# Two units of an input projection moved into the stage that prepares its input

## The reference, cut to what matters

```
u = _rmsnorm(h, w['g_mix'][i])                     # 1536 tokens x 1024
proj = u @ w['w_in'][i]                            # columns: q, k, v, z, xbc, dt
q, k, v, z, xbc, dt = jnp.split(proj, [o1, o2, o3, o4, o5], axis=-1)
...
gates = jax.nn.sigmoid(u @ w['w_gate'][i] + w['b_gate'][i])
```

## Time and profile before

| | |
|---|---|
| median of 3 runs | 2904.48 us (2902.88 to 2906.73) |
| profiled execution, own time | 2904.54 us |
| its span | 2902.9 us |
| TensorE (PE) busy, share of the span | 92% |
| VectorE (DVE) / ScalarE (ACT) busy | 53% / 44% |

### The profile page before, as it was taken

How to read it: one execution, slowest core, us unless ns; L and a number is a source line. 1 busy time by engine, 2 the same in 40 slices (tenths; PEclk the granted TensorE clock), 3 DMA queues, 4 the chain that set the end, 5 groups by cost and what they waited for, 6 DMA issues and landing times. The chain is left out here.

```text
span 2902.9 us, 40069 instructions
## 1 busy us (share of the span) xinstructions
PE 2677.1 (92%) x15166; PEld 2287.9 (79%) x15166; DVE 1548.2 (53%) x2049; ACT 1287.9 (44%) x1766; POOL 312.7 (11%) x301
## 2 busy tenths in 40 slices
PE   5999999999998885996998986999999999999798
PEld 3889888778877672665887875999999999999686
DVE  6000000072108777896763266677677767776555
ACT  5111111143217887555542124555555555555454
POOL 1000000010001200221110012000110011101021
PEclk9999999999999997998999987999999999999899
DMA  4422121165323304336885546787888788778532
GB/s 148 111 73 73 72 108 60 50 209 183 117 84 104 99 16 137 121 104 191 264 266 209 188 160 207 249 250 237 244 257 250 238 243 260 246 238 245 176 137 80
DMA packets 412315, 486.55 MB, mean 168 GB/s; under 512 B 17576, under 2 KB 359480, under 8 KB 411208
## 3 DMA queue, kind: packets, MB, share of 16 engines
q1 hardware_dynamic: 386880, 383.80, 42.0%
q0 software_dynamic: 25328, 101.30, 11.0%
HBM read 378.68 MB, written 106.36 MB: 167 GB/s over the span
## 5 line engine op out<-in xcount | busy, mean ns | idle before, releaser
L2174 DVE TENSOR_TENSOR ex_w_lo<-ex_w_raw,ex_w_hi 128x2048 fp32r<-128x2048 f32 x195 | 443.9, 2291 | 142.8 <-ACT ex_w_hi L2131 142.8
L2263 PE MATMUL ex_ps_u<-ex_x,ex_w_hi 128*128 128x384 f32 x2048 | 411.2, 341 | 5.1 <-DVE ex_w_lo L2174 5.1
L2131 ACT ACTIVATE ex_w_hi<-ex_w_raw 128x2048 fp32r<-128x2048 f32 x195 | 370.4, 1909 | 0.8
L2263 PEld LDWEIGHTS ex_ps_u<-ex_x,ex_w_hi 128*128 128x128 f32 x2048 | 348.8, 189 | 6.2 <-issue 5.5
L2263 PEld LDWEIGHTS ex_ps_u<-ex_x,ex_w_lo 128*128 128x128 f32 x2048 | 265.5, 191 | 0.6
L2282 PE MATMUL ex_ps_d<-ex_w_hi,ex_h 128*128 128x512 f32 x768 | 265.9, 400 | 0.0
L2263 PE MATMUL ex_ps_u<-ex_x,ex_w_lo 128*128 128x192 f32 x2048 | 265.4, 272 | 0.0
L358 DVE TENSOR_TENSOR w_lo<-w_raw,w_hi 128x2048 fp32r<-128x2048 f32 x14 | 32.1, 2292 | 404.2 <-ACT w_hi L324 404.2
L330 ACT ACTIVATE stage<-ps 128x512 f32<-128x512 f32 (+1 forms) x102 | 55.8, 547 | 402.6 <-PE ps L382 347.1
L2282 PE MATMUL ex_ps_d<-ex_w_lo,ex_h 128*128 128x512 f32 x512 | 202.9, 396 | 0.0
L2148 ACT ACTIVATE ex_beside<-ex_ps_u 128x384 f32<-128x384 f32 x128 | 62.9, 492 | 248.6 <-PE ex_ps_u L2263 248.6
(11 more groups left out here) (401 smaller groups left out, 4806.8 us busy)
## 6 DMA issues: line engine op xcount, KB each, us to landing
ex_w_raw<-in_w_exp_gate SPq DMA_DIRECT2D x64, 1024.0 KB, 5.4
ex_w_raw<-in_w_exp_up SPq DMA_DIRECT2D x64, 1024.0 KB, 6.3
ex_w_raw<-in_w_exp_down SPq DMA_DIRECT2D x64, 1024.0 KB, 6.4
w_raw<-in_w_in SPq DMA_DIRECT2D x15, 1024.0 KB, 5.3
g_d<-gst SPq DMA_DIRECT2D x48, 256.0 KB, 2.0
mg_w_raw<-in_w_ssm_up SPq DMA_DIRECT2D x24, 512.0 KB, 5.6
mg_g_raw<-g_d SPq DMA_DIRECT2D x24, 512.0 KB, 7.3
gw_raw<-in_w_gate SPq DMA_DIRECT2D x16, 512.0 KB, 5.6
```

The costliest lines, as they stand in the source:

```text
L2131: act.activation(unit(w_hi, j), w_raw[:, j % RAW], ACT.Copy).then_inc(w_hi_done, 1)
L2174: dve.tensor_tensor(unit(w_lo, j), w_raw[:, j % RAW], unit(w_hi, j).bitcast(F32), ALU.subtract).then_inc(w_split, 1)
L2263: last = pe.matmul(ps_u[:, j % 2, m, 0:wide * C], w[:, s // 2, k, s % 2, cols], x[:, k, 0:wide].rearrange("p a c -> p (a c)"), start=i == ...
```

## The change

Units 0 and 1 of q/k (12 groups) are computed in stage 1. The groups run block by block of 512 tokens; group 0 may start once tiles 0 to 3 have their `u_lo`. TensorE's order is: turns 0 and 1, the four bias-line products in a row, turns 2 to 4, then one group, one turn, one group, and so on to turn 11, then the last five groups (7 to 11). Four PSUM banks take the groups in rotation (before, they held the bias line). ScalarE copies each group to a two-slot `qk_stage`, and SP stores each by itself, 256 KB. Stage 1 now also loads and splits unit 1's weights, and at its end unit 2's, with which `project` begins. The bias line's copy moves from tile 6 to tile 1, the split of unit 0's weights from tiles 4 and 7 to tiles 2 and 3. `project` keeps two units of q/k. In core:

```
-    SPLIT_HI, LINE_COPY, SPLIT_LO = 4, 6, 7
+    LEAD = BLK // P
+    HI_AT, LO_AT = {2: 0, 5: 1}, {3: 0, 5: 1}
+    GROUPS = [(u, m, b) for b in range(NB) for u in range(2) for m in range(WC // P)]
+    LAST_OF_0 = max(g for g, (u, _, _) in enumerate(GROUPS) if u == 0) + 1
...
+        ps_g = ctx.enter_context(nc.psum_tensor("nu_ps_g", [P, 4, BLK], F32))
+        ps_line = ps_g[0:MAPS]
...  SP
             sp.wait_ge(x_in[1], 16)
+            sp.dma_start(w_raw[:, 0], w_view[:, :, 0:WC]).then_inc(w_landed[0], 16)
+            sp.wait_ge(line_made, LINE // BLK)
+            sp.dma_start(w_raw[:, 1], w_view[:, :, WC:2 * WC]).then_inc(w_landed[1], 16)
+            sp.wait_ge(w_split, 1)
+            sp.dma_start(w_raw[:, 0], w_view[:, :, 2 * WC:3 * WC]).then_inc(w_landed[0], 16)
+            for g, (u, m, b) in enumerate(GROUPS):
+                sp.wait_ge(copied, g + 1)
+                sp.dma_start(qk_out[u, m][:, b * BLK:(b + 1) * BLK], qk_stage[:, g % 2]).then_inc(qk_stored[g % 2], 16)
...  ScalarE
+            def evacuate(g):
+                act.wait_ge(full, g + 1)
+                if g >= 2:
+                    act.wait_ge(qk_stored[g % 2], 16 * (g // 2))
+                act.activation(qk_stage[:, g % 2], ps_g[:, g % 4], ACT.Copy).then_inc(copied, 1)
...  in its loop over tiles, after u_hi
+                if n in HI_AT:
+                    act.wait_ge(w_landed[HI_AT[n]], 16)
+                    act.activation(w_hi[:, HI_AT[n]], w_raw[:, HI_AT[n]], ACT.Copy).then_inc(w_hi_done, 1)
+                if n == 1:
                     act.wait_ge(line_made, LINE // BLK)
+                    act.activation(line, ps_line...)
+                if n > LEAD:
+                    evacuate(n - LEAD - 1)
...  after it: the other copies, and between them w_hi of unit 2
...  VectorE, after u_lo
+                if n in LO_AT:
+                    dve.wait_ge(w_hi_done, LO_AT[n] + 1)
+                    dve.tensor_tensor(w_lo[:, LO_AT[n]], ..., ALU.subtract).then_inc(w_split, 1)
...  TensorE
+            def product(g):
+                u, m, b = GROUPS[g]
+                if g % (NG // NB) == 0:
+                    pe.wait_ge(lo_done, LEAD * (b + 1))
+                if g < 4:
+                    pe.wait_ge(w_split, u + 1)
+                if g == 0:
+                    pe.wait_ge(line_copied, 1)
+                if g >= 4:
+                    pe.wait_ge(copied, g - 3)
+                terms = ...            # the 24 matmuls of channels_first
...
             for b in range(LINE // BLK):
                 pe.matmul(ps_line[:, b], ...)
-                turn(b + 2)
-            for n in range(LINE // BLK + 2, TT):
+            for n in range(2, TT):
                 turn(n)
+                if n >= LEAD:
+                    product(n - LEAD)
+            for g in range(TT - LEAD, NG):
+                product(g)
...  project
-    U_QK, U_V, U_Z, U_X = 2 * QKW // WC, VW // WC, D // WC, D // WC
+    U_QK, U_V, U_Z, U_X = 2 * QKW // WC - 2, VW // WC, D // WC, D // WC
```

More of the change, by code:

```diff
@@ L108, in bucket_one_hot, with turn_and_split @@
     return (bucket[None, :] == np.arange(BUCKETS)[:, None]).astype(np.float32)
-def turn_and_split(nc, rows, gain_row, ident, u_hi, u_lo, w_in, table, one_hot, w_raw, w_hi, w_lo, line):
+def turn_and_split(nc, rows, gain_row, ident, u_hi, u_lo, w_in, table, one_hot, w_raw, w_hi, w_lo, line, qkT_d, qk_stage, qk_stored):
     W = rows.shape[-1]
@@ L120, in turn_and_split @@
     MAPS = 2 * HEADS
-    SPLIT_HI, LINE_COPY, SPLIT_LO = 4, 6, 7
+    LEAD = BLK // P
+    HI_AT, LO_AT = {2: 0, 5: 1}, {3: 0, 5: 1}
+    GROUPS = [(u, m, b) for b in range(NB) for u in range(2) for m in range(WC // P)]
+    NG = len(GROUPS)
+    LAST_OF_0 = max(g for g, (u, _, _) in enumerate(GROUPS) if u == 0) + 1
+    qk_out = qkT_d.rearrange("(u m p) t -> u m p t", p=P, m=WC // P)
+    w_view = w_in.rearrange("(k p) c -> p k c", p=P)
     with ExitStack() as ctx:
@@ L130, in turn_and_split @@
         ps = ctx.enter_context(nc.psum_tensor("nu_ps", [P, 2, K, P], F32))
-        ps_line = ctx.enter_context(nc.psum_tensor("nu_ps_line", [MAPS, LINE // BLK, BLK], F32))
+        ps_g = ctx.enter_context(nc.psum_tensor("nu_ps_g", [P, 4, BLK], F32))
+        ps_line = ps_g[0:MAPS]
         consts_in, set_up, x_in = sem("consts_in"), sem("set_up"), [sem("x_in%d" % r) for r in range(RING)]
@@ L135, in turn_and_split @@
         line_in, line_made, line_copied = sem("line_in"), sem("line_made"), sem("line_copied")
-        w_landed, w_hi_done, w_split = sem("w_landed"), sem("w_hi_done"), sem("w_split")
+        w_landed, w_hi_done, w_split = [sem("w_landed0"), sem("w_landed1")], sem("w_hi_done"), sem("w_split")
+        full, copied = sem("full"), sem("copied")
         block = open_block(nc, ctx)
@@ L152, in _ @@
             sp.wait_ge(x_in[1], 16)
-            sp.dma_start(w_raw[:, 0], w_in.rearrange("(k p) c -> p k c", p=P)[:, :, 0:WC]).then_inc(w_landed, 16)
+            sp.dma_start(w_raw[:, 0], w_view[:, :, 0:WC]).then_inc(w_landed[0], 16)
[6 more added lines that the diff above has]
+                sp.dma_start(qk_out[u, m][:, b * BLK:(b + 1) * BLK], qk_stage[:, g % 2]).then_inc(qk_stored[g % 2], 16)
         @block.scalar
@@ L173, in _ @@
                 act.activation(u_hi[:, :, n * P:(n + 1) * P], ps[:, n % 2], ACT.Copy).then_inc(hi_done, 1)
[L174 to L177, removed]
+                if n in HI_AT:
+                    act.wait_ge(w_landed[HI_AT[n]], 16)
+                    act.activation(w_hi[:, HI_AT[n]], w_raw[:, HI_AT[n]], ACT.Copy).then_inc(w_hi_done, 1)
+                if n == 1:
                     act.wait_ge(line_made, LINE // BLK)
-                    act.activation(line, ps_line[:].rearrange("p b c -> p (b c)"), ACT.Copy, scale=-1.0).then_inc(line_copied, 1)
+                    act.activation(line, ps_line.rearrange("p b c -> p (b c)"), ACT.Copy, scale=-1.0).then_inc(line_copied, 1)
+                if n > LEAD:
+                    evacuate(n - LEAD - 1)
+            for g in range(TT - LEAD - 1, LAST_OF_0):
+                evacuate(g)
+            act.wait_ge(w_landed[0], 32)
+            act.wait_ge(full, LAST_OF_0)
+            act.activation(w_hi[:, 0], w_raw[:, 0], ACT.Copy).then_inc(w_hi_done, 1)
+            for g in range(LAST_OF_0, NG):
+                evacuate(g)
         @block.vector
@@ L204, in _ @@
                 dve.tensor_tensor(u_lo[:, :, n * P:(n + 1) * P], ps[:, n % 2], u_hi[:, :, n * P:(n + 1) * P].bitcast(F32), ALU.subtract).then_inc(lo_done, 1)
-                if n == SPLIT_LO:
-                    dve.wait_ge(w_hi_done, 1)
-                    dve.tensor_tensor(w_lo[:, 0], w_raw[:, 0], w_hi[:, 0].bitcast(F32), ALU.subtract).then_inc(w_split, 1)
+                if n in LO_AT:
+                    dve.wait_ge(w_hi_done, LO_AT[n] + 1)
+                    dve.tensor_tensor(w_lo[:, LO_AT[n]], w_raw[:, LO_AT[n]], w_hi[:, LO_AT[n]].bitcast(F32), ALU.subtract).then_inc(w_split, 1)
+            dve.wait_ge(w_hi_done, 3)
+            dve.tensor_tensor(w_lo[:, 0], w_raw[:, 0], w_hi[:, 0].bitcast(F32), ALU.subtract).then_inc(w_split, 1)
         @block.tensor
@@ L218, in turn @@
                 last.then_inc(turned, 1)
+            def product(g):
[8 more added lines that the diff above has]
+                    pe.wait_ge(copied, g - 3)
+                terms = [(w, v, k) for w, v in ((w_hi, u_hi), (w_lo, u_hi), (w_hi, u_lo)) for k in range(K)]
+                for i, (w, v, k) in enumerate(terms):
+                    last = pe.matmul(ps_g[:, g % 4], w[:, u, k, m * P:(m + 1) * P], v[:, k, b * BLK:(b + 1) * BLK], start=i == 0, stop=i == len(terms) - 1)
+                last.then_inc(full, 1)
             pe.wait_ge(consts_in, 32)
@@ L225, in _, with project @@
                 pe.matmul(ps_line[:, b], tab[:], hot[:, b * BLK:(b + 1) * BLK], start=True, stop=True).then_inc(line_made, 1)
-                turn(b + 2)
-            for n in range(LINE // BLK + 2, TT):
+            for n in range(2, TT):
                 turn(n)
-def project(nc, u_hi, u_lo, w_in, w_raw, w_hi, w_lo, line, ident, qkT_d, v_d, zgT_d, xbcT_d, dt_d, line_d, w_gate, gate_tiles, gw_raw, gw_hi, gw_lo):
+                if n >= LEAD:
+                    product(n - LEAD)
+            for g in range(TT - LEAD, NG):
+                product(g)
+def project(nc, u_hi, u_lo, w_in, w_raw, w_hi, w_lo, line, ident, qkT_d, v_d, zgT_d, xbcT_d, dt_d, line_d, w_gate, gate_tiles, gw_raw, gw_hi, gw_lo, qk_stored):
     WC, RING = WIN, 6
@@ L241, in project @@
     w_view = w_in.rearrange("(k p) c -> p k c", p=P)
-    C_QK, C_V, C_Z, C_X, C_DT = 0, 2 * QKW, 2 * QKW + VW, 2 * QKW + VW + D, 2 * QKW + VW + D + XBC
+    C_QK, C_V, C_Z, C_X, C_DT = 2 * WC, 2 * QKW, 2 * QKW + VW, 2 * QKW + VW + D, 2 * QKW + VW + D + XBC
     NDT = 2 * SH
     G_CH, G_TOK = (WC // P) * NB, TT
-    U_QK, U_V, U_Z, U_X = 2 * QKW // WC, VW // WC, D // WC, D // WC
-    qk_out = qkT_d.rearrange("(u m p) t -> u p m t", p=P, m=2)
```

(11 more changed lines are left out.)

## The result

The changed kernel takes 2883.34 us, the median of 4 runs (2879.66 to 2889.0), against 2903.78 for the kernel before beside it (4 runs, 2902.88 to 2906.73): a ratio of 0.9932, interval 0.9919 to 0.9946. That is 20.4 us less where 16.2 was forecast, and inside the range of 2882 to 2897. The four runs fall into two pairs (2879.66 and 2879.8, 2886.88 and 2889.0), and the median lies between them.

The account below looks back on a forecast made before the run. Stage 2 was taken as bound by its matmuls, stage 1 by passing tiles between engines. Unit 2 starting at 111.8 instead of 128.0 gains 16.2 us: 2904.5 - 16.2 = 2888.3 us, range 2882 to 2897.

Parts of the forecast that it names:

- The start of group 0: Stage 1: group 0 starts at 36.3 us, right after the low part of unit 0's weights, bounds 32.7 to 38.6.
- The lower bound of 32.7: Stage 1: group 0's start if the row of bias products ran at the fast level, ending 3.6 us earlier.
- The rival that it belongs to: Stage 1: group 0 starts early (bias products fast, 3.6 us) or fast (no slow start, 1.7): 2883 to 2887; chance 0.08.
- Group 0 was mis-sized: Stage 1: group 0 costs 7.1 us from a slow clock, bounds 5.44 if already fast and 7.44 as in stage 2.
- The alternation: Stage 1 after group 0: 7 turns at 0.9 us and 11 groups taking 59.84 us, with TensorE not held up.
- The tiles did not set the pace: Stage 1 rival: tiles, not matmuls, set the pace; waits in three steps lose 7 us, giving 2895; chance 0.11.
- the slack: Stage 1: unit 1's weights are ready at 49.7 us, group 2 is due at 50.6, leaving 0.9.
- The clock stayed up in stage 1: Stage 1: groups run fast after group 0; the rival of 1.2 GHz throughout gave near 2958 us, chance 0.05.
- that rule: Stage 1: cycling PSUM banks could make the clock swing; by it the sum would be the second rival's, near 2958 us.
- The hand-over: Stage 1 to `project`: last copy, store and engine join take 2.3 us, so unit 2 starts at 111.8.
- Each as long as before: Blocks after stage 1: all stand some 16 us earlier, with their lengths unchanged.

Follow-up runs that it names:

- the first profile: The changed kernel as first profiled, against the kernel before: 2889.0 us, the longest of its four runs.
- the second and third: The changed kernel profiled twice more with nothing edited: own times 2879.34 us and 2883.75 us.
- the first pair: First profile of the kernel before (2904.54 us) and first profile of the changed kernel (2889.0 us).
- the third experiment: Changed kernel with the four bias products laid back between the turns and ScalarE's copy of the line moved to tile 3: 2877.34 us, ratio 0.9909.
- the fill: Eight unused matmuls behind stage 1's last group, added to the changed kernel with bias products between turns: 2879.5 us, ratio 0.9916.

## Why the prediction was right

**The start of group 0 held:** 36.60 in place of 36.3, with the row of four bias products on the path as worked out; its first turn came 0.55 later than in before (12.46 against 11.91), which is scatter (11.43 to 12.46 in the profiles of changed kernels). The lower bound of 32.7, with the products at the fast level, was a real case: 32.69 and 32.70 in two profiles. The rival that it belongs to was given 0.08, and it was seen in 2 of the 7 profiles that have the four in a row; seven profiles do not settle how frequent it is. With it, convolve starts at 555.8 in place of 561.5 and 562.4.

**Group 0 was mis-sized:** 7.1 forecast, upper bound 7.44, measured 8.23 in the first profile (36.60 to 44.83), 7.17 and 7.88 in the second and third. In the first its second eight matmuls still took 2.84, the third 1.84; the clock rose within the second, later than in the last block, whose row I had taken. With this and group 0's start 0.3 late, unit 2 started at 113.07, 1.3 later than the 111.8 forecast.

**The alternation held:** from 44.83 to the last group's end, 105.58 + 5.44 = 111.02, it took 66.2, forecast 66.1. The tiles did not set the pace: no idle time in that stretch. Unit 1's low part ended at 48.76 + 2.29 = 51.05, 0.93 ahead of group 2, and the slack had been put at 0.9.

**The clock stayed up in stage 1:** 1.00 over 66.1 us, with four banks in rotation. The swinging of the clock that the Trainium skill (TensorE: Matmul & The Clock Gate, "A second HAM failure mode: psum-queue depth-cycling") describes did not come. There the engine idles briefly between groups of matmuls; here it had no idle time (66.10 of 66.10), so this case does not test that rule.

**The hand-over held:** 113.07 - 111.02 = 2.05 (2.3 forecast). The clock fell in it in this profile, at 7.17 - 5.44 = 1.7 for the first group; the prediction had allowed 2.0 and kept it out of the sum.

**"Each as long as before" failed** for the later blocks. They took 5.3 us less in the mean of three profiles each, 4.0 of it in attention, 2.5 of that directly in the wait for its loads of q and k; by the run times of before it is nearer to 3. So the gain of 20.4 is about 17 us of start (576.6 - 559.9 in the mean of three profiles each, forecast 16.2) and some 3 of later blocks. In single executions the parts shift: 14.0 and 1.6 in the first pair. That the mean start comes so near to the forecast is partly luck: in the first and third profiles convolve starts 14.2 and 15.1 before the mean of before, 2.0 and 1.1 less than forecast, and only the short row of the second (20.8) lifts the mean. That the start is due to the overlap is shown: without it convolve started at 579.2 and the median was only 3.3 below before.

**Open:** why these loads land later in before, and in the third experiment. It is not where in the span attention starts (with all turns ahead of the groups at 867.8, close to the 866.3 of before, and yet 220.9 us long), nor the queue of the new stores. That the waits make the later blocks of the two kernels differ is likely from the profiles, but not shown by the medians. Open too is why the same row of bias products is short in some executions.

## What to carry to other kernels

Work moved into a stage in which TensorE waits for other engines can fill those waits: here stage 1 grew by 52.4 us (60.3 to 112.7) for groups that had taken 67.3 in `project`. What decides is when the first group can start, so look at what stands in TensorE's and ScalarE's order ahead of it. Here four products moved into one row put up to 7 us on that path, and laying them back between the turns let group 0 start some 5 us earlier. When a gain differs from the sum, compare the lengths of blocks that were not touched in several executions of both kernels before giving them a cause, and hold the profiles against the spread of the run times.

## What the runs showed of the hardware

Identical code met different clocks. The four bias products in a row (eight records in the trace) took 6.99 us in five profiles and 3.79 and 3.63 in two, although the turns behind them took 1.97 in both kinds (19.50 in the second profile of after, at a granted clock of 0.50). With the ten extra matmuls of 128x384 the clock did rise ahead of group 0: behind the first six, which took 2.00 us, a turn took 1.09 in place of 1.97.

The pause at the hand-over let the clock fall in four profiles (1.89 or 1.92 us; `project` 449.7 to 450.2 us) and not in four others (1.89 in three, 1.54 with the stores on POOL; 448.0 to 448.2), and a pause of 1.72 had left it up in the earlier trace rows. Filled to 0.81 and 0.80 it stayed up in both profiles that had the fill, too few to say that the fill did it.

The clock printed for the start of a profile is 1.00 in a stretch where eight transposes take 1.94 (0.50 is printed where they take as long in the earlier trace rows), so a stretch's clock is to be held against durations there.
